# A chunked scan in a decoder trunk: packed transposes, half-copied keys, and queries and state decays on GpSimd

## The reference, cut to what matters

```
def hgrn2: S_t = diag(g_t) S_{t-1} + k_t v_t^T,  o_t = S_t^T q_t      (decays g_t per key channel)
def gated_delta: S_t = exp(g_t)(I - beta_t k_t k_t^T) S_{t-1} + beta_t k_t v_t^T,  o_t = S_t^T q_t
    # within a chunk: sol = triangular_solve(eye + akk, rhs), a unit lower triangular system
```

## Time and profile before

| | before |
|---|---|
| median of 3 runs | 1004.21 us (1003.80 to 1004.48) |
| the profiled execution's own time | 1004.29 us |
| its span, first to last instruction | 1002.4 us |
| TensorE busy | 990.8 us (99%) |
| VectorE busy | 664.7 us (66%) |
| ScalarE busy | 514.4 us (51%) |
| GpSimd busy | 98.0 us (10%) |
| mean granted clock of TensorE | 0.999 |

### The profile page before, as it was taken

How to read it: one execution, slowest core, us unless ns; L and a number is a source line. 1 busy time by engine, 2 the same in 40 slices (tenths; PEclk the granted TensorE clock), 3 DMA queues, 4 the chain that set the end, 5 groups by cost and what they waited for, 6 DMA issues and landing times.

```text
span 1002.4 us, 21125 instructions
## 1 busy us (share of the span) xinstructions
PE 990.8 (99%) x8326; PEld 977.7 (98%) x8326; DVE 664.7 (66%) x907; ACT 514.4 (51%) x727; POOL 98.0 (10%) x158
## 2 busy tenths in 40 slices
PE   9999999999999999999999999999999999999998
PEld 8999999999998889999999999999999999999998
DVE  6766565589887977766654486666546986666443
ACT  7544443476785746444443474444336364444334
POOL 6800000010021202000000020000001030000001
PEclk9999999999999999999999999999999999999999
DMA  7565566655454525655555555556554546566551
GB/s 257 195 210 185 187 207 213 197 169 171 146 163 132 171 71 183 189 188 189 187 178 186 184 182 197 190 191 206 187 189 130 166 143 197 172 193 191 181 186 44
DMA packets 49755, 177.98 MB, mean 178 GB/s; under 512 B 5945, under 2 KB 5961, under 8 KB 49681
## 3 DMA queue, kind: packets, MB, share of 16 engines
q1 hardware_dynamic: 46224, 165.50, 50.4%
q0 software_dynamic: 3184, 11.35, 3.8%
q10 hardware_dynamic: 288, 0.32, 0.1%
HBM read 171.19 MB, written 6.52 MB: 177 GB/s over the span
## 4 chain that ended last, share of the span: by engine, by line
PE 90%; DVE 6%; ACT 2%; issue 1%; DMA 1%; POOL 0%; SPq 0%; DVEq 0%; ACTq 0%; POOLq 0%
PE ps L1808 28%; PE ps L1810 28%; PE ps L1809 28%; DVE w_lo L1268 1%; DMA raw<-in_ffn_w_gate 1%; DVE PT L1227 1%; PE ps L1600 1%; ACT xw_hi L624 0%; PE ps L1631 0%; DVE rstd L1295 0%; PE ps L1606 0%; POOL hn L1993 0%; ACT w_hi L614 0%; DVE xw_lo L1289 0%; DVE hn L1233 0%
## 5 line engine op out<-in xcount | busy, mean ns | idle before, releaser
L614 ACT CAST w_hi<-raw 128x1024 fp32r<-128x1024 f32 x309 | 321.5, 1046 | 408.3 <-PE ps L1810 406.6
L1268 DVE TENSOR_TENSOR w_lo<-raw,w_hi 128x1024 fp32r<-128x1024 f32 x309 | 374.7, 1228 | 180.2 <-ACT w_hi L614 178.0
L1808 PE MATMUL ps<-xw_hi,w_hi 128*128 128x264 f32 x1472 | 418.6, 284 | 2.2 <-DVE w_lo L1268 1.5
L1809 PE MATMUL ps<-xw_lo,w_hi 128*128 128x264 f32 x1472 | 416.6, 283 | 0.0
L1810 PE MATMUL ps<-xw_hi,w_lo 128*128 128x264 f32 x1472 | 416.6, 283 | 0.0
L1808 PEld LDWEIGHTS ps<-xw_hi,w_hi 128*128 128x128 f32 x1472 | 276.7, 188 | 4.5 <-DVE w_lo L1268 2.4
L1809 PEld LDWEIGHTS ps<-xw_lo,w_hi 128*128 128x128 f32 x1472 | 276.8, 188 | 0.1
L1810 PEld LDWEIGHTS ps<-xw_hi,w_lo 128*128 128x128 f32 x1472 | 276.7, 188 | 0.0
L1808 PE MATMUL ps<-a_hi,w_hi 128*128 128x264 f32 x704 | 199.2, 283 | 0.0
L1809 PE MATMUL ps<-a_lo,w_hi 128*128 128x264 f32 x704 | 199.2, 283 | 0.0
L1810 PE MATMUL ps<-a_hi,w_lo 128*128 128x264 f32 x704 | 199.2, 283 | 0.0
(11 more groups left out here) (369 smaller groups left out, 749.0 us busy)
## 6 DMA issues: line engine op xcount, KB each, us to landing
raw<-in_ffn_w_up SPq DMA_DIRECT2D x88, 512.0 KB, 4.1
raw<-in_ffn_w_down SPq DMA_DIRECT2D x88, 512.0 KB, 4.2
raw<-in_ffn_w_gate SPq DMA_DIRECT2D x87, 512.0 KB, 4.2
raw<-in_w_in_even SPq DMA_DIRECT2D x32, 512.0 KB, 3.5
raw<-in_w_out_even SPq DMA_DIRECT2D x8, 512.0 KB, 3.6
raw<-in_pool_w_in SPq DMA_DIRECT2D x8, 512.0 KB, 4.1
out<-SBUFS POOLq DMA_DIRECT2D x4, 512.0 KB, 3.4
x<-in_x SPq DMA_DIRECT2D x4, 264.0 KB, 5.3
```

Source lines behind the costliest of these rows:

```text
L614: nc.scalar.copy(w_hi[:, w % SPL, :], raw[:, w % RAW, :]).then_inc(hi_done, 1)
L1268: nc.vector.tensor_tensor(w_lo[:, w % SPL, :], raw[:, w % RAW, :], w_hi[:, w % SPL, :].bitcast(F32), ALU.subtract).then_inc(lo_done, 1)
L1808: mm(out, wh, hi, start=first, stop=False)
L1809: mm(out, wh, lo, start=False, stop=False)
```

## The change

1. **Inverse.** In turns 2 to 5 ScalarE first copies the columns of T that the level needs, from both chunks, into a packed tile TP (512 elements), and TensorE makes four transposes of TP in place of eight of T. ScalarE copies the result with one copy of 512 elements in place of two of 256. TensorE's transposes now wait for the packing copy. Turn 6 keeps its eight.
2. **Keys.** The keys for the next level, KP, are no longer packed by one ScalarE copy after the multiply. ScalarE copies the half that the level doesn't change (`kept_keys`, 256 elements, after attention of the turn), and VectorE writes the other half itself, as a product of KS and totals (`fresh_keys`, 256 elements, `hg_fresh`). VectorE still multiplies KS in place (`level_keys`), now behind `new_state`.
3. **Queries** (`level_queries`, 512 elements) are multiplied by GpSimd.
4. **Decays** of states 4 to 7 are one GpSimd multiply of 1024 elements each, in turns 1, 2, 4 and 5, behind the queries and ahead of the turn's store.
5. **VectorE's order**: the attention merge of level 0 comes behind the T merge of turn 1, and the two weight splits come behind the last addition to HS2. In turns 2 to 6 the order is merge_att, merge T, half write, new state, key multiply.

```diff
@@
-READ = {1: 4, 2: 5, 4: 6, 5: 7}
+POOL_DECAY = {1: 4, 2: 5, 4: 6, 5: 7}
@@
-        HS1, HS2, KP = XL[:, 0:512], XL[:, 512:1024], XL[:, 1024:1536]
+        HS1, HS2, KP, TP = XL[:, 0:512], XL[:, 512:1024], XL[:, 1024:1536], XL[:, 1536:2048]
@@
+        def level_views(keys, l):
+            half = 1 << l
+            n = 512 // half
+            a = KS if keys else QG
+            y = 1 if keys else 0
+            s = 1 - 2 * y
+            if l == 0:
...
+            else:
+                t = total(l - 1)
+                out = both(KS[:, 0:512], 512 + half, l) if keys else both(QG[:, half:half + 512], 512 - half, l)
+                by = bass.AP(t.tensor, t.offset + y, [list(t.ap[0]), [n + s, 2], [2, n // 2], [0, half]])
+            return out, out, by
+
+        def fresh_keys(l):
+            half = 1 << l
...
+                out, old = [bass.AP(a.tensor, a.offset, [list(a.ap[0]), [step, 2], [4 * half, 512 // (4 * half)], [1, half]])
+                            for a, step in ((KP, 3 * half), (KS, 512 + 3 * half))]
+                by = bass.AP(t.tensor, t.offset + 1, [list(t.ap[0]), [512 // half + 1, 2], [4, 512 // (4 * half)], [0, half]])
+            return out, old, by
+
+        def kept_keys(l):
+            half = 1 << l
+            return [bass.AP(a.tensor, a.offset + half, [list(a.ap[0]), [step, 2], [4 * half, 512 // (4 * half)], [1, half]])
+                    for a, step in ((KP, half), (KS, 512 + half))]
@@ scalar
             for l in range(1, LEVELS):
+                if 1 < l < LEVELS - 1:
+                    act.wait_ge(st("inv_tc"), l)
+                    A.copy(TP.rearrange("p (j two r) -> p j two r", two=2, r=1 << l), both(TU[:, 0:4, :].rearrange("p i n -> p (i n)"), 512 + (1 << l), l, True))\
+                        .then_inc(st("inv_pack"), 1)
                 act.wait_ge(st("inv_x"), l)
...
                 if l > 1:
                     act.wait_ge(st("inv_u"), l - 1)
-                    for side, bank in ((0, psV), (1, psT)):
-                        if l < LEVELS - 1:
-                            ins = A.copy(tiles(UP, l, side), tiles(bank, l, side))
-                        else:
-                            ins = A.copy(U[:, 4 * side:4 * side + 4, :], bank)
+                    if l < LEVELS - 1:
+                        ins = A.copy(UP, psV)
+                    else:
+                        A.copy(U[:, 0:4, :], psV)
+                        ins = A.copy(U[:, 4:8, :], psT)
                     ins.then_inc(st("inv"), 1)
+                act.wait_ge(st("hg_att"), l + 1)
+                if l > 1:
+                    act.wait_ge(st("hg_k"), l - 1)
+                kept, old = kept_keys(l - 1)
+                A.copy(kept, old).then_inc(st("hg_pack"), 1)
...
-                if l in READ:
-                    decay_state(READ[l])
...
-                if l < LEVELS - 1:
-                    act.wait_ge(st("hg_k"), l)
-                    pack(l)
@@ vector
             def level_update(l):
...
-                V.tensor_tensor(k4, k4, rb, ALU.mult).then_inc(st("hg_k"), 1)
-                V.tensor_tensor(q4, q4, lb, ALU.mult).then_inc(st("hg_lvl"), 1)
+                if l:
+                    dve.wait_ge(st("hg_k"), l)
+                if l < LEVELS - 1:
+                    V.tensor_tensor(*fresh_keys(l), ALU.mult).then_inc(st("hg_fresh"), 1)
+                    new_state(l + 1)
+                    dve.wait_ge(st("hg_fresh"), l + 1)
+                V.tensor_tensor(*level_keys(l), ALU.mult).then_inc(st("hg_k"), 1)
+                if l == LEVELS - 1:
+                    new_state(l + 1)
 
             def new_state(j):
-                dve.wait_ge(st("samp_dec"), j + 1)
+                dve.wait_ge(*((st("samp_dec"), j + 1) if j < 4 else (st("hg_dec"), j - 3)))
...
                 if 1 <= r < LEVELS:
-                    dve.wait_ge(st("hg_lvl"), r - 1)
-                    dve.wait_ge(st("hg_merge"), r + 1)
-                    dve.wait_ge(st("hg_att"), r + 1)
-                    merge_att(r - 1).then_inc(st("hg_merge"), 1)
+                    if r > 1:
+                        dve.wait_ge(st("hg_lvl"), r - 1)
+                        dve.wait_ge(st("hg_merge"), r + 1)
+                        dve.wait_ge(st("hg_att"), r + 1)
+                        merge_att(r - 1).then_inc(st("hg_merge"), 1)
                     dve.wait_ge(st("inv_t"), r)
...
-                    if r == LEVELS:
+                    if r in (1, LEVELS):
...
-                if r in (4, 5):
-                    tick(S_PROJ + 26 + r)
...
             V.tensor_tensor(HS2, HS2, ps[:, 3, :], ALU.add).then_inc(st("hs2"), 1)
+            tick(S_PROJ + 30)
+            tick(S_PROJ + 31)
@@ tensor
-                if 2 <= r < LEVELS:
+                if 2 <= r < LEVELS - 1:
+                    pe.wait_ge(st("inv_pack"), r - 1)
+                    for h in range(4):
+                        ins = tr(psV[:, h, :], TP[:, h * P:(h + 1) * P], ident[:, :])
+                    ins.then_inc(st("inv_u"), 1)
+                if r == LEVELS - 1:
...
                     if r > 1:
+                        pe.wait_ge(st("hg_fresh"), r - 1)
                         pe.wait_ge(st("hg_lvl"), r - 1)
...
-                    pe.wait_ge(st("samp_dec"), 6 + 2 * y)
+                    pe.wait_ge(st("hg_dec"), 2 + 2 * y)
@@ gpsimd
             for j in range(8):
+                if j:
+                    pool.wait_ge(st("hg_att"), j + 1)
+                    if j > 1:
+                        pool.wait_ge(st("hg_lvl"), j - 1)
+                    G.tensor_tensor(*level_queries(j - 1), ALU.mult).then_inc(st("hg_lvl"), 1)
+                if j in POOL_DECAY:
+                    i = POOL_DECAY[j]
+                    pool.wait_ge(st(f"samp_in{i if i < 6 else i - 6}"), 16 if i < 6 else 32)
+                    G.tensor_tensor(SV(i), SV(i), GG[:, i - 4, PROMPT:TOK].unsqueeze(2).broadcast_to([P, NSAMP, P]), ALU.mult)\
+                        .then_inc(st("hg_dec"), 1)
                 pool.wait_ge(st("samp_new"), j + 1)
```

More of the change, by code:

```diff
@@ L304, in both, with level_keys, level_queries @@
             return bass.AP(a.tensor, a.offset, [list(a.ap[0])] + dims)
+        def level_views(keys, l):
[5 more added lines that the diff above has]
+            if l == 0:
+                out = bass.AP(a.tensor, a.offset + 1 - y, [list(a.ap[0]), [512 - s, 2], [P, 4], [2, P // 2]])
+                by = bass.AP(GG, GG[:, :, :].offset + y, [list(GG[:, :, :].ap[0]), [P + s, 2], [TOK, 4], [2, P // 2]])
+            else:
[3 more added lines that the diff above has]
+            return out, out, by
+        def level_keys(l):
+            return level_views(True, l)
+        def fresh_keys(l):
+            half = 1 << l
+            if l == 0:
+                out, old = [bass.AP(a.tensor, a.offset, [list(a.ap[0]), [step, 2], [P, 4], [4, P // 4]]) for a, step in ((KP, 3), (KS, 515))]
+                by = bass.AP(GG, GG[:, :, :].offset + 1, [list(GG[:, :, :].ap[0]), [P + 1, 2], [TOK, 4], [4, P // 4]])
+            else:
+                t = total(l - 1)
+                out, old = [bass.AP(a.tensor, a.offset, [list(a.ap[0]), [step, 2], [4 * half, 512 // (4 * half)], [1, half]])
[6 more added lines that the diff above has]
+                    for a, step in ((KP, half), (KS, 512 + half))]
+        def level_queries(l):
+            return level_views(False, l)
         @block.sync
@@ L440, in decay_state @@
             def decay_state(j):
-                act.wait_ge(st(f"samp_in{j if j < 6 else j - 6}"), 16 if j < 6 else 32)
-                h = j % 4
+                act.wait_ge(st(f"samp_in{j}"), 16)
                 for b in range(NSAMP):
-                    col = SMALL[:, 96 + 8 * h + b:97 + 8 * h + b] if j < 4 else GG[:, h, PROMPT + b:PROMPT + b + 1]
+                    col = SMALL[:, 96 + 8 * j + b:97 + 8 * j + b]
                     ins = A.activation(SV(j)[:, b, :], SV(j)[:, b, :], ACT.Identity, scale=col)
@@ L495, in read_rows @@
                 A.copy(HREADS[y], ps[:, 7, 0:128]).then_inc(st("read_rows"), 1)
-            def pack(l):
-                A.copy(KP.rearrange("p (j two r) -> p j two r", two=2, r=1 << l), both(KS[:, 0:512], 512 + (1 << l), l, True))\
-                    .then_inc(st("hg_pack"), 1)
             act.wait_ge(st("hg_att"), 1)
-            pack(0)
+            A.copy(KP.rearrange("p (j two) -> p j two", two=2), both(KS[:, 0:512], 512 + 1, 0, True).rearrange("p j two r -> p j (two r)"))\
+                .then_inc(st("hg_pack"), 1)
             for l in range(1, LEVELS):
+                if 1 < l < LEVELS - 1:
+                    act.wait_ge(st("inv_tc"), l)
+                    A.copy(TP.rearrange("p (j two r) -> p j two r", two=2, r=1 << l), both(TU[:, 0:4, :].rearrange("p i n -> p (i n)"), 512 + (1 << l), l, True))\
+                        .then_inc(st("inv_pack"), 1)
                 act.wait_ge(st("inv_x"), l)
@@ L510, in even_scalar @@
                     act.wait_ge(st("inv_u"), l - 1)
[L511 to L516 removed]
```

(28 more changed lines are left out.)

2 lines of the change are left out of this document (removed).

## The result

The changed kernel takes 1007.15 us (median of eight executions, 1006.63 to 1007.6) beside 1004.14 for the kernel before on the same chip (eight, 1003.66 to 1004.72): ratio 1.0029, 95% interval 1.0019 to 1.0039. It is 3 us slower. The profiled execution took 1006.63 (span 1004.5).

What follows compares the result with a forecast made beforehand. In the 35 us scan TensorE and VectorE are both nearly full, most turns ending on one or the other. Without collisions -0.4 us, plus 3.35 of waits, gives +2.9 on 1004.29: 1007.2 us, range 1003.2 to 1010.

Steps and rivals of the forecast that it cites:

- a case that had 0.66: Scan: GpSimd's multiplies and VectorE operations with two SBUF inputs exclude each other as placed, +2.9 us in sum; chance 0.66.
- Four transposes: TensorE in the scan: four transposes in place of eight save 0.44 us in a turn that TensorE sets.
- Turn 2 without a collision: VectorE's round in turn 2 grows from 5.03 to 5.46 us, as two double-priced attention copies move into it.
- Turn 3: Half write slips between queries and decay; the decay holds the key multiply 1.2 us; turn 5.1 against 4.41, +0.7.
- Turn 4: Queries begin as VectorE asks, so it waits 1.15 us in a round it sets, 5.3 us without the wait.
- Turn 5: GpSimd's decay holds VectorE's half write 1.1 us; turn 4.5 against 4.41, +0.1.
- Behind turn 6: The new state waits for its outer product ahead of the keys, which costs 0.3 us.
- The splits: VectorE's two weight splits, 2 x 1.13 us, fit a 2.58 us hole before the gating and cost nothing.
- The signs: X products of turns 3 to 6 and state product 1.7 to 3 us later; half writes, key multiplies 1.5 to 2.
- A: Rival: GpSimd's and VectorE's operations don't meet, only -0.4 us is left, 1003.8; chance 0.15.
- C: Rival: VectorE's merges are held too, or short runs slow GpSimd; every turn waits 0.5 to 1 more, 1010 to 1013; chance 0.08.
- B: Rival: VectorE's work sets every turn, so its net loss of 4.4 us counts in full, 1000 us or so; chance 0.11.

Runs made afterwards that it cites:

- e7: The kernel before with the packed transposes alone, keys packed by ScalarE behind the new packing copy: 1003.46 us, ratio 0.9992.
- f1: The changed kernel with only the decays of states 4 to 7 put back on ScalarE; queries stay on GpSimd: 1004.89 us, ratio 1.0006.
- e8: The changed kernel with turn 1's two small key and value copies made by ScalarE in place of VectorE: 1006.90 us, ratio 1.0029.
- e3: The changed kernel with ScalarE's gate and its table load moved ahead of turn 3's half copy of kept keys: 1006.50 us, ratio 1.0021.
- g1: f1 with ScalarE's gate ahead of turn 3's half copy and the key multiply ahead of turn 6's state update: 1004.13 us, ratio 0.9999.
- f2: The kernel before with packed transposes and the two weight splits moved behind the scan, no queries or decays on GpSimd: 1003.02 us, ratio 0.9988.
- b1: The kernel before with packed transposes, splits behind the scan, small copies on ScalarE and decays on GpSimd, keys and queries on VectorE: 1005.65 us, ratio 1.0018.
- e6: The changed kernel with queries back on VectorE behind the key multiply, decays staying on GpSimd from the turn's attention: 1010.87 us, ratio 1.0065.
- e4: The changed kernel with small key/value parts ahead of attention merge, gate ahead of kept keys, and GpSimd's decays waiting for the half write: 1006.77 us, ratio 1.0023.
- e2: The changed kernel with VectorE's small key and value parts of turn 1 moved ahead of the attention merge: 1008.57 us, ratio 1.0043.
- f3: f1 with the queries also taken off GpSimd, on VectorE right behind the half write: 1005.50 us, ratio 1.0013.
- e5: The changed kernel with GpSimd's four decays replaced by memsets of the same tiles, which read nothing: 1007.38 us, ratio 1.0022.

## Why the prediction was right

1007.2 was predicted, 1007.15 measured, in a case that had 0.66. The mechanism is shown: the two engines exclude each other when both read SBUF and VectorE takes two inputs from it, and with the decays off GpSimd 2.36 of 2.76 us are back. The turns, though, are not all as the prediction built them. Step by step:

- *Four transposes.* Predicted -0.44 in turns 3 and 5. Alone (e7) they gave -0.46 in turn 3 and -0.16 in turn 5, where the split still stood in VectorE's row; with the split gone -0.45. Right.
- *Turn 2 without a collision*, predicted 5.46: f1 has 5.49. With the 1.4 of waiting 6.86: 6.75 measured. The half write took 1.70 where f1 has 0.64, so it waited 1.06 and not 1.4; 0.31 of the turn is the small copy's wait, which was not foreseen (e8). The collision is right, the near-exact total is not all its doing.
- *Turn 3*, predicted: "the half write slips in between queries and decay (0.4, hidden)", and the key multiply waits 1.2; turn about 5.1. Wrong. The half write waited for both and took 2.88, and the key multiply nothing. GpSimd's decay starts 0.05 before the queries have ended (323.02 + 1.32 against 324.29), which fits that there was no place to slip in. The turn was 5.72: the term of +0.7 should have been about +1.3.
- *Turn 4*, predicted: VectorE's half write waits 1.15 for queries. It started 0.27 before the queries of 329.74 and took 0.45. In its place TensorE waited 0.90 for the packing copy behind the gate. The prediction had said of this copy that it "could be late if ScalarE were still decaying, but the decays have left it", and had not looked at the gate. With e3's order the turn is 5.37, near the 5.3 that the prediction had without a wait. The predicted wait does come in f1 and g1 (0.8), where the queries start earlier. The turn was +0.49 against 5.60 before (the prediction read 5.5) in place of +0.95, from another cause: turn 3's error and this one, of opposite sign, nearly cancel.
- *Turn 5*, predicted: the decay holds the half write for 1.1, turn 4.5. It took 1.61, so it was held for about 1.2, but the turn was 4.30. *Turn 6*, predicted: the key multiply waits 1.2 behind the last decay, hidden. Hidden is right (turn 6 is 9.96 without decays too, in f1), but as in turn 3 it was the half write, 2.29 behind queries and decay.
- *Behind turn 6*, predicted +0.3 for the state update's wait ahead of the keys: +0.46, and g1 shows that this order is the cause.
- *GpSimd's durations.* Decays 1.9 and not 2.5, near the lower bound of 1.8; queries 1.04 to 1.51 (1.3). The half write is 0.41 to 0.45, and 0.64 to 0.68 in turn 2, where 0.35 was taken.
- *The splits* cost nothing behind the scan: 15.08 beside 15.07, and f2 the same. Right.
- *The signs.* Counted from the start of the scan, the X products of turns 3 to 6 come 1.39, 2.26, 2.75 and 2.30 later and the state product 2.76, where 1.7, 2.2, about 3, about 3 and 3 were named. It is half writes that show 1.6 to 2.9 us; no key multiply does.
- *Rivals.* A (no meeting) and C (held merges) are out: the predicated merges that start under a GpSimd multiply take their 0.4 to 0.8, as before. B overrated VectorE's relief: e7 and f2 have the most that any run here gained, 1.0 us in the scan.

So the cause was right and the total in part luck. With decays of 1.9 the prediction's own placing would have given a sum between its lower bound and its middle (1005.3 to 1007.2); what made up for it are the half write that waits for queries and decay together, and the gate.

## What to carry to other kernels

Before work is moved to GpSimd, list what VectorE does meanwhile with two inputs in SBUF: every multiply of GpSimd that meets one of these runs before or after it and not beside it. A change of order helps only where GpSimd's multiply then lies under VectorE operations with an input from PSUM (one decay in b1), and it must not put a result that TensorE wants at the end of the row (e6); otherwise the wait moves to another operation (e4). Count GpSimd's multiplies that follow each other without a gap as one block. And take apart a change with many parts: here the transposes and the moved splits shorten the scan by 1.0 us (f2), the decays on GpSimd lengthen it by 2.4 (f1), the place of the key multiply in turn 6 by another 0.5 to 0.6 (g1), and about 0.9 belong to the rest of the change, which no run took apart.

## What the runs showed of the hardware that was not expected

- A GpSimd multiply that follows another directly leaves the half write no gap: it took 2.88 us in place of 0.41 to 0.45 behind queries and decay (3.04 in e8, 2.29 in turn 6). The Trainium skill, "SBUF — State Buffer", section "Summary: rules for kernel authors", says that the second to issue is blocked until the first finishes; here it waited for two.
- What holds what differs by form. The VectorE copy of 64 elements from SBUF to SBUF was held by GpSimd's multiplies (2.44 in e2, 0.57 in e4), and in five runs under a DMA issue (1.59 in the changed kernel and e3, 1.61 in g1, 0.56 in f3, 3.76 in e5). But an issue doesn't hold it always: the copy just ahead of it took 0.16 to 0.19 under the same issue in all five, and in f1 and e6 neither was held. No run shows what decides this. A VectorE operation with two SBUF inputs was held by no issue and by no memset (0.67, 0.41 and 0.42 under a memset, 0.45 with a load issue under way, 0.18 for the small subtractions in e8), only by GpSimd's multiplies. Merges and state updates with an input from PSUM kept their times under these multiplies.
- The copy's hold doesn't stop the next starts: behind L991 the merges start at their usual pace (321.83, 322.33), and only their ends pile up at 323.11. The half write's hold does stop the row: behind 323.61 the next start is 326.41.
- TensorE's granted clock fell in turns 2 and 3 of the three profiled executions with its longest pauses there (e2: 0.84 and 0.82 behind 2.81 us, e5: 0.74 behind 3.06, e6: 0.72 behind 2.39), and stayed at 1.00 in the changed kernel, whose waits are at most 1.35. In these traces the wait costs TensorE more than its length (eight attention products took 2.05 in e2, where the changed kernel has 1.15). The whole times don't settle how much: e5's four executions with a mean clock of 0.999 or more are at least 1.86 us faster than its others, but e2's two with 1.000 (1008.56 and 1008.58) are as slow as its two with 0.997 and 0.998.
